# First layer's output projection: from fp32 matmuls to three fp32r passes over split operands

## The reference, cut to what matters

```
y_a = o_a * silu(g_a)                                   # attention, 1024 columns
y_m = (h_m + skip * x_c) * silu(z_m)                    # mLSTM, 1024 columns
y = concatenate([y_a, y_m], axis=-1) @ w_out            # (256, 2048) @ (2048, 1024)
return x + rmsnorm(y, g_post)
```

## Time and profile before

| | |
|---|---|
| median of 3 runs | 2116.25 us (2115.89 to 2117.53) |
| profiled execution | 2117.82 us, its span 2115.7 us |
| busy PE / DVE / ACT | 97% / 73% / 58% of the span |
| the eight chunks of the projection | from 224.75 to 324.60 us of the span, within the attention steps |

### The profile page before, as it was taken

How to read it: one execution, slowest core, us unless ns; L and a number is a source line. 1 busy time by engine, 2 the same in 40 slices (tenths; PEclk the granted TensorE clock), 3 DMA queues, 4 the chain that set the end, 5 groups by cost and what they waited for, 6 DMA issues and landing times.

```text
span 2115.7 us, 29766 instructions
## 1 busy us (share of the span) xinstructions
PE 2051.0 (97%) x10242; PEld 1670.0 (79%) x10242; DVE 1537.6 (73%) x2103; ACT 1225.2 (58%) x1597; POOL 42.1 (2%) x52
## 2 busy tenths in 40 slices
PE   8999999899999999999988999999999999999998
PEld 6687658758998777999755888888888888888887
DVE  6256626686664765554266989989898989989898
ACT  2211226544443455443254878888888878888886
POOL 0000000000000000000100000000000000000000
PEclk9999999999999999999989999999999999999999
DMA  9667744326553315555214999999999999999996
GB/s 317 171 227 255 268 163 165 100 80 223 175 194 125 100 53 186 188 191 160 90 60 174 401 388 369 384 361 395 357 401 358 400 381 368 393 355 395 348 409 243
DMA packets 275470, 548.71 MB, mean 259 GB/s; under 512 B 29493, under 2 KB 81214, under 8 KB 275134
## 3 DMA queue, kind: packets, MB, share of 16 engines
q1 hardware_dynamic: 266189, 528.46, 68.4%
q0 software_dynamic: 3984, 14.68, 2.3%
q10 hardware_dynamic: 5216, 4.49, 0.8%
HBM read 537.11 MB, written 10.48 MB: 259 GB/s over the span
## 4 chain that ended last, share of the span: by engine, by line
PE 92%; DVE 5%; ACT 1%; DMA 1%; issue 1%; SPq 0%; DVEq 0%; ACTq 0%
PE sum L1559 12%; PE bank L727 10%; PE bank L1541 10%; PE bank L1543 10%; PE bank L1542 10%; PE sum L1183 6%; PE sum L789 6%; PE bank L1200 3%; PE bank L1202 3%; PE bank L1201 3%; PE bank L743 1%; PE sum L1290 1%; PE bank L1527 1%; DMA relrow<-arena 1%; PE sum L1573 1%; PE sum L769 1%
## 5 line engine op out<-in xcount | busy, mean ns | idle before, releaser
L2962 DVE TENSOR_TENSOR x_lo<-ring,x_hi 128x1024 fp32r<-128x1024 f32 x672 | 780.2, 1220 | 43.9 <-ACT x_hi L2096 24.5
L2096 ACT ACTIVATE x_hi<-ring 128x1024 fp32r<-128x1024 f32 x648 | 667.0, 1058 | 119.1 <-PE bank L1543 66.0
L1541 PE MATMUL bank<-x_hi,hg_hi 128*128 128x512 f32 x896 | 354.2, 395 | 1.6 <-DVE xtr L2919 1.6
L1543 PE MATMUL bank<-x_hi,hg_lo 128*128 128x512 f32 x896 | 349.4, 390 | 0.0
L1542 PE MATMUL bank<-x_lo,hg_hi 128*128 128x512 f32 x896 | 348.9, 389 | 0.0
L2304 DVE TENSOR_TENSOR w_lo<-ring,w_hi 128x1024 fp32r<-128x1024 f32 x130 | 158.0, 1225 | 114.6 <-ACT w_hi L1906 112.8
L727 PE MATMUL bank<-hT,ring 128*128 128x256 f32 x1024 | 230.8, 387 | 2.6 <-DVE hT L2337 1.8
L727 PEld LDWEIGHTS bank<-hT,ring 128*128 128x128 f32 x1024 | 198.3, 194 | 35.1 <-issue 7.6
L1906 ACT ACTIVATE w_hi<-ring 128x1024 fp32r<-128x1024 f32 x130 | 136.6, 1058 | 147.8 <-PE bank L1202 76.5
L1543 PEld LDWEIGHTS bank<-x_hi,hg_lo 128*128 128x128 f32 x896 | 168.1, 188 | 35.8
L1541 PEld LDWEIGHTS bank<-x_hi,hg_hi 128*128 128x128 f32 x896 | 168.3, 188 | 34.9 <-DVE xtr L2919 1.7
(11 more groups left out here) (497 smaller groups left out, 2739.6 us busy)
## 6 DMA issues: line engine op xcount, KB each, us to landing
ring<-in_sw_we_gate SPq DMA_DIRECT2D x114, 1024.0 KB, 7.3
ring<-in_sw_we_up SPq DMA_DIRECT2D x112, 1024.0 KB, 7.4
ring<-in_sw_we_down SPq DMA_DIRECT2D x112, 1024.0 KB, 7.3
ring<-in_w_in SPq DMA_DIRECT2D x36, 1024.0 KB, 7.4
ring<-in_w_ff SPq DMA_DIRECT2D x32, 1024.0 KB, 5.3
ring<-in_ada_w SPq DMA_DIRECT2D x24, 1024.0 KB, 7.2
ring<-in_w_out SPq DMA_DIRECT2D x12, 1024.0 KB, 7.4
ring<-in_cv_w_gate SPq DMA_DIRECT2D x11, 1024.0 KB, 5.1
```

The source lines that it names most:

```text
L1541: mm(ps[b][:, :], hg_hi[:, k, :], hi[:, cols], start=(k == 0), stop=False)
L1543: last = mm(ps[b][:, :], hg_lo[:, k, :], hi[:, cols], start=False, stop=(k == KC - 1))
L2096: go(f(x_hi[:, hp % MSLOTS, :], ring[:, s, lo:lo + PIECE // 2], ACT.Copy), c.sig("hi_ready", hp))
L2962: v.tensor_tensor(x_lo[:, hp % MSLOTS, :], ring[:, s, lo:lo + PIECE // 2], x_hi[:, hp % MSLOTS, :].bitcast(F32), ALU.subtract).then_inc(c. ...
```

## The change

The eight chunks go through three fp32r passes. ACT writes the high part of chunk k (`rows_high(k)`, two instructions of 128x1024) into a ring slot that is reserved for it: `split_rows` gives each `w_out` chunk a second number in SP's order, for which nothing is transferred, so each chunk holds two of the seven slots. DVE subtracts in place (`rows_low(k)`, two instructions of 128x1024). The concatenated outputs are split where they are made: after each `mix_heads(q)` a copy and a subtraction of 128x512, after each attention head a copy and a subtraction of 128x256; the high parts lie in `mix1_hi` (parts of the arena and of `nrm`), the low parts over `mix1`. PE's `b1_out(k)` waits for `mix_split` and, by half chunk, for `rows_low`. Slots are freed when PE is done with the chunk, both together. The placement is given by `B1_SPLIT`; chunk 4 has its calls ahead of step 0, on DVE after `ada(8)`, on ACT after the value copies.

```diff
+B1_SPLIT = {1: 5, 3: 6, 4: 7, 5: 0, 6: 1, 8: 2, 9: 3}
+            def split_rows(name, w, k):
+                chunk_rows(name, w, k)
+                n = W.n
+                W.n += 1
+                W.number[name + "_hi", k] = n
+                W.landing[name + "_hi", k] = (n % RING, W.slot[n % RING])
...
             def b1_out(k):
-                sum_rows("b1", "w_out", 8, mix1, mixed, (k,), first=4, last_=3)
+                pe.wait_ge(*c.at("mix_split", k))
+                hi, lo = (ring_r[:, W.place((name, k)), :].rearrange("p (k n) -> p k n", k=2) for name in ("w_out_hi", "w_out"))
+                for t in range(NT):
+                    for h in range(2):
+                        for j in range(2):
+                            if t + h == 0:
+                                pe.wait_ge(*c.at("rows_low", k, j))
+                            m_hi, m_lo = (x[:, t * P:(t + 1) * P] for x in (mix1_hi[2 * k + j], mix1_lo[:, 2 * k + j, :]))
+                            cs = slice(h * 512, (h + 1) * 512)
+                            mm(acc[2 * t + h][:, :], m_hi, hi[:, j, cs], start=(k == 4 and j == 0), stop=False)
+                            mm(acc[2 * t + h][:, :], m_hi, lo[:, j, cs], start=False, stop=False)
+                            last = mm(acc[2 * t + h][:, :], m_lo, hi[:, j, cs], start=False, stop=(k == 3 and j == 1))
...
+                free([("w_out", k), ("w_out_hi", k)], s)
...
+            def rows_high(k):
+                key = ("w_out", k)
+                act.wait_ge(*W.ready(key))
+                act.wait_ge(*W.vacated(("w_out_hi", k)))
+                for j in range(2):
+                    cs = slice(j * D, (j + 1) * D)
+                    go(f(ring_r[:, W.place(("w_out_hi", k)), cs], ring[:, W.place(key), cs], ACT.Copy), c.sig("rows_high", k, j))
             for col in (2048, 2560):
                 for t in range(NT):
                     copy(vt[:, t, col - 2048:col - 2048 + 512], ("b1v", col, t))
+            rows_high(4)
             for i in range(HEADS1 + 3):
...
                         copy(pair(mix1, q - 12), ("b1p", q), func=ACT.Silu)
+                if i in B1_SPLIT:
+                    rows_high(B1_SPLIT[i])
                 if 2 <= i < HEADS1 + 2:
                     probs_T("b1", i - 2, T384, "b1O")
...
+                heads = slice(8 + 2 * q, 10 + 2 * q)
+                split(nrm_r[:, :, q * S:(q + 1) * S], mix1_lo[:, heads, :], mix1[:, heads, :], c.sig("mix_split", 4 + q))
...
+            def rows_low(k):
+                for j in range(2):
+                    dve.wait_ge(*c.at("rows_high", k, j))
+                    cs = slice(j * D, (j + 1) * D)
+                    x, hi = W.place(("w_out", k)), W.place(("w_out_hi", k))
+                    v.tensor_tensor(ring_r[:, x, cs], ring[:, x, cs], ring_r[:, hi, cs].bitcast(F32), ALU.subtract).then_inc(c.sig("rows_low", k, j).sem, 1)
             mix_heads(2)
             mix_heads(3)
             ada(8)
+            rows_low(4)
...
                 if i == 5:
                     ada(11)
+                if i in B1_SPLIT:
+                    rows_low(B1_SPLIT[i])
                 if i >= 3:
...
-                    do(v.tensor_tensor(mix1[:, h, :], mix1[:, h, :], bank("b1O", h)[:, 0:S], ALU.mult), J.free("b1O", h))
+                    do(v.tensor_tensor(x, x, bank("b1O", h)[:, 0:S], ALU.mult), J.free("b1O", h))
+                    split(mix1_hi[h], mix1_lo[:, h, :], x, c.sig("mix_split", h // 2) if h % 2 else None)
```

More of the change, by code:

```diff
@@ L285, in ffn_used, with vacated @@
         return self.c.sem(name), v
+    def vacated(self, key):
+        name, v = self.known.freed[self.known.number[key] - RING] if self.known else ("piece_used", 1)
+        return self.c.sem(name), v
     def place(self, key):
@@ L325, in program @@
         ident, ones = C("ident"), C("ones")
+        with ExitStack() as phase:
+            ring_r = phase.enter_context(nc.sbuf_tensor("ring_r", [P, RING, PIECE], F32R))
         ring = sb("ring", RING, PIECE)
         xres = sb("xres", NT, D)
+        with ExitStack() as phase:
+            nrm_r = phase.enter_context(nc.sbuf_tensor("nrm_r", [P, NT, D], F32R))
         nrm = sb("nrm", NT, D)
@@ L372, in sp_ @@
                 return phase.enter_context(nc.sbuf_tensor(name, [P, *shape], dt))
-            sp_("units_0_to_5", 6 * 1024, dt=F32)
+            sp_("units_0_and_1", 2 * 1024, dt=F32)
+            mix1_lo = sp_("mix1_lo", 16, S)
             d_lo = sp_("d_lo", SPLIT_SLOTS, PIECE // 2)
-            sp_("units_9_to_15", 7 * 1024, dt=F32)
+            sp_("units_9_to_11", 3 * 1024, dt=F32)
+            mix1_hi = sp_("mix1_hi", 8, S)
+            sp_("units_14_and_15", 2 * 1024, dt=F32)
             d_hi = sp_("d_hi", SPLIT_SLOTS, PIECE // 2)
@@ L427, in program @@
         mix1 = U(2, 16, S)
+        mix1_hi = [mix1_hi[:, h, :] for h in range(8)] + [nrm_r[:, j, q * S:(q + 1) * S] for q in range(4) for j in range(2)]
         relbias = U(6, HEADS1, 384)
@@ L559, in ffn @@
                         columns(name, weights[name], 256 * g, 256)
+            def split_rows(name, w, k):
[4 more added lines that the diff above has]
+                W.landing[name + "_hi", k] = (n % RING, W.slot[n % RING])
             for i, g in enumerate(B1_ORDER):
                 if g == 3072:
-                    chunk_rows("w_out", A["w_out"][0], 4)
+                    split_rows("w_out", A["w_out"][0], 4)
                 columns("w_in", A["w_in"][0], g)
@@ L579, in _ @@
                 if g == 3072:
-                    chunk_rows("w_out", A["w_out"][0], 5)
+                    split_rows("w_out", A["w_out"][0], 5)
             for k in (6, 7, 0, 1, 2, 3):
-                chunk_rows("w_out", A["w_out"][0], k)
+                split_rows("w_out", A["w_out"][0], k)
             if upto >= 2:
@@ L982, in _ @@
                     pe.wait_ge(*J.emptied("b1v", col, t))
[L984 to L990, removed]
-            def b1_out(k):
-                sum_rows("b1", "w_out", 8, mix1, mixed, (k,), first=4, last_=3)
+            def b1_out(k):
+                pe.wait_ge(*c.at("mix_split", k))
[10 more added lines that the diff above has]
+                            last = mm(acc[2 * t + h][:, :], m_lo, hi[:, j, cs], start=False, stop=(k == 3 and j == 1))
+                        if k == 3 and t + h < 2:
+                            last.then_inc(c.sig("sums", "b1", 2 * t + h).sem, 1)
+                s = c.sig("piece_used", "b1", k)
+                last.then_inc(s.sem, 1)
+                free([("w_out", k), ("w_out_hi", k)], s)
             def b1_between(i):
@@ L2485, in _ @@
                     dve.wait_ge(*J.emptied("b1p", 12 + h // 2))
-                    do(v.tensor_tensor(mix1[:, h, :], mix1[:, h, :], bank("b1O", h)[:, 0:S], ALU.mult), J.free("b1O", h))
+                    x = mix1[:, h, :]
+                    do(v.tensor_tensor(x, x, bank("b1O", h)[:, 0:S], ALU.mult), J.free("b1O", h))
+                    split(mix1_hi[h], mix1_lo[:, h, :], x, c.sig("mix_split", h // 2) if h % 2 else None)
             for o, name in ((8, "mix_norm_g_2"), (24, "ffn_norm_g_2")):
```

## The result

The changed kernel is slower: 2133.14 us median of 4 runs (2128.48 to 2134.16) against 2116.64 us, a ratio of 1.0069 (95% interval 1.0057 to 1.0081), about 14.6 us (the two medians themselves lie 16.5 us apart). I had forecast 2126.2 us, 10 us slower, with a range up to 2130. The sign was right and the size too small. The profiled execution took 2132.91 us, its span 2130.9.

The account below looks back on a forecast made before the run. PE, busy 97% of the span, was taken to bound the kernel. Terms 8.2 + 0.5 + 9.9 - 11.2 + 0.6 + 2.0 made 10.0 us slower, forecast 2126.2 us, range 2119.5 to 2130.

Parts of the forecast that it names:

- The saving: Projection chunks: three fp32r passes take 5.47 us against 6.87, saving 1.40 us a chunk, 11.2 us for eight.
- The first chunk: Ahead of chunk 4, PE waits 8.2 us for DVE's burst, then 0.5 us for the second half chunk.
- The clock in chunk 4: After the long first wait PE starts chunk 4 at half clock, losing 2.0 us.
- The other seven chunks: Chunks 5, 6, 7, 0, 1, 2 and 3: PE's added waits for splits cost 9.9 us together.
- The ring: Chunks hold two slots, so some w_in pieces go out later; counted as nothing, 1 to 2 us if last in queue.
- The tail: After chunk 3, DVE is still in the first token tile when the last sum is there: 0.6 us lost.
- The sum for the stage: All terms of the projection stage added: 10.0 us slower.
- The clock that stays up: Rival: after the first wait the clock stays up or returns at once, 2124.2 us; chance 0.17.
- the late ring piece: Rival: the second w_in 3584 piece comes 2 us late and PE waits in step 3, 2128.2 us; chance 0.15.
- the short later waits: Rival: the seven later chunks' waits shrink to 2.4 us, 2118.7 us, no change that can be told; chance 0.10.
- the burst that isn't in front of chunk 4: Rival: DVE ends rows_low(4) by 224.9, so first wait and clock loss go, 2108.0 us, faster; chance 0.06.
- the clock step's bound: Half clock at chunk 4 after the first wait: loss between nothing and 3.4 us, 2.0 taken.

Follow-up runs that it names:

- order: Changed kernel with chunk 4 left fp32 and unsplit, the other seven chunks' splits moved in ACT's and DVE's order: 2116.11 us, ratio 0.9999.
- best: On top of order, products with the even head's half go first in chunks 0 to 2, in chunk 3 for two of four banks: 2109.50 us, ratio 0.9962.
- defer: Changed kernel with the splits of mLSTM heads 2 and 3 moved behind logits(0), out of DVE's burst ahead of chunk 4: 2126.43 us, ratio 1.0046.
- fill: Changed kernel with 17 fp32 matmuls of 128x256 put into PE's wait ahead of chunk 4: 2129.61 us, ratio 1.0056.
- delay3: Kernel before plus three DVE subtractions of 128x1024 after ada(8), for which PE waits ahead of chunk 4: 2127.37 us, ratio 1.0038.
- ring_only: Kernel before with only the change's slot reservation, matmuls still fp32 and nothing split: 2118.81 us, ratio 1.0004.
- before_again: Kernel before run again without edit, for a second trace: 2115.03 us, ratio 0.9995.
- delay: Kernel before plus seven DVE subtractions of 128x1024 after ada(8), for which PE waits ahead of chunk 4: 2136.85 us, ratio 1.0083.

## Why the prediction was right and wrong, step by step

**The saving**, put at 1.40 us a chunk: 1.26 in the run order, 10.1 us for eight and not 11.2. Mis-sized by 1.1 us. Here the products start 0.233 us apart, in the row I took it from the earlier trace rows 0.228. That row has another order of banks, and its products share a stationary operand two by two. In the changed kernel six products in a row go to one bank; in best it is three, and the distance is 0.233 all the same. So the run of six is not what makes the difference, and its cause stays open.

**The first chunk**, put at 8.2 + 0.5 us: 8.12 by the trace. The end of `rows_low(4)`'s first half was forecast for 232.9 and came at 233.2. That DVE's burst sets it is shown by defer.

**The clock in chunk 4**, put at 2.0: the chunk took 8.28, 7.85 and 8.04 us in the three traces of the changed kernel and 6.05 in fill, so 1.8 to 2.2. Both halves of the step are shown: the wait alone brings it (delay3), work in the wait removes it.

**The other seven chunks**, put at 9.9 us beyond before's waits: the waits read 1.74, 0.74, 0.68, 0.55, 0.57, 1.37 and 1.71, 7.4 us, less 1.4 that were there before, with up to 0.4 us each in chunks 5, 6, 7 and 0 for the second half (6.04 from start to end, against 5.6 unhindered). That makes about 7.7 us. I overcounted by 2, most of it at chunks 1 and 7 (0.6 and 0.5). That their cause is order and not amount is shown for chunks 5, 6, 7, 0 and 1; for chunk 2 it is amount as well, and the wait ahead of chunk 3 changed only when the even head's products went first (best).

**The ring**, nothing: right, shown by ring_only.

**The tail**, put at 0.6 us: 1.4 to 1.9 us in the three traces of the changed kernel, against the undisturbed 11.03. The longer wait for DVE, 0.4 us, is of the forecast size. The fall of the clock behind it was not in the forecast. Against the first trace of the kernel before, the tail seems to cost nothing, because that trace had such a fall too.

**The sum for the stage** was 10.0 us. The first two traces make it 9.65, which looks like a hit; against the undisturbed stage it is 10.9. In part the nearness is luck: the waits of the seven chunks were put 2 us too high and the saving 1.1 us too high, and the fall at 330 us in the base hid the loss in the tail. The measured terms up to the end of chunk 3 are 8.1 for the first wait, 2.7 for chunk 4 (8.28 against 5.6, the clock's 2.2 in it), 7.7 for the others and 1.0 for an overlap: each bracket leaves out the 0.16 us by which a product that doesn't wait overlaps the one ahead of it, and there are six new waits. Less 10.1 of saving that is 9.4, and the trace has 9.49. With 0.34 us that was there ahead of the stage and 0.18 less in the tail this makes the 9.65.

**The rivals.** The clock that stays up is out (0.50 in the windows above), the late ring piece is out, the short later waits were half right, and the burst that isn't in front of chunk 4 is out.

**What failed** is the clock step's bound, and with it the top of the range. It said that the loss to the clock "lies between nothing and 3.4 us", as if only chunk 4 could pay. Chunk 4 paid as forecast. But the clock also fell in the stage's tail, in all three traces of the changed kernel, and at about 386 and 1160 us in two of the three. The runs of the upper heap, to which these two belong, are those outside the range; the seven of the lower heap, 2125.6 to 2128.5, lie in it. The rest of the span took 1784.0 us in the changed kernel's first trace and 1778.45 before, with the same instructions. Over all thirteen traces here it lies between 1775.7 (before_again) and 1784.1 us (fill), and the four largest are the four with falls around 1160 us: first and third trace of the changed kernel, fill, delay. One profiled execution gave me a base that I took as exact, while two traces of the kernel before differ by 5.1 us in span, 1.6 of them inside the stage.

**What stays open.** Over 16 runs the changed kernel is 13.4 us over before (2130.7 against 2117.3, the mean of the runs of before beside them), 2.5 us more than the 10.9 of its stage. The lower heap of its runs is 10.0 us over before's mean, about what the stage costs; the upper heap, 16.1 us over, is one that the kernel before hardly has (two of its 38 runs beside these are above 2120 us). Why the falls around 1160 us came in two of three traces of the changed kernel and in none of the two of before is not settled. delay shows that they need no three-pass matmul; delay3, late by 9.1 us, did not have them, and its mean had no excess. Nor is it a longer wait: in all thirteen traces PE comes there with the same waits for DVE and ACT, 0.84, 0.52, 0.61 and 1.10 us before the first of the two falls, to 0.01 us. That the falls depend on exactly when the work arrives there is argued, not shown. An experiment that keeps PE at work at that place was not run.

## What to carry to other kernels

A rest of an engine is room only for work that stands inside the rest in the engine's own order and depends on nothing later: the three passes cost 14 us in one order, and in another, with one chunk of eight left out, they gained 8. Ahead of a new wait, list what the awaited engine does from its last forced stop; that list predicted 8.1 us to a tenth. And let the products whose operands are oldest go first, so that the last split hides behind them.

## What the runs showed of the hardware

A PE wait of 8.1 us cost 1.8 to 2.5 us more through half clock in what followed, and one of 5.7 us also brought it (chunk 4 of defer took 7.79 us). Smaller waits sometimes did and sometimes not: after the 3.3 us in order and after 1.7 us at 257 us in fill the clock fell, in the changed kernel's own traces a wait of the same 1.7 us passed without. Ahead of the next block a wait of 2.05 us was followed by half clock in one trace of five, one of 2.5 us in seven of seven. So two traces of one kernel differ by 5.1 us in span (before) or 7.4 (changed), with the same long waits in the stage. A change's effect is better read between a mark close ahead of it and one close behind it than at the end, and against more than one trace of the kernel before. The Trainium skill (page TensorE: Matmul & The Clock Gate, section What's actually happening) says that activity releases the throttle; fill agrees, with a granted clock of 1.00 where the changed kernel had 0.50.
